# Sparse attention in a tuned model kernel: probabilities scaled before they are turned, values stationary, three branches in one bank

## The reference

```python
for each block of 128 queries, for each of 8 heads (2 groups G of 4):
    p_cmp = masked_softmax(q @ k_cmp * scale)        # 31 compressed keys
    o_cmp = p_cmp @ v_cmp
    p_sel = masked_softmax(q @ k_selected * scale)   # 16 blocks of 64 keys
    o_sel = p_sel @ v_selected
    p_win = masked_softmax(q @ k_window * scale)     # the last 512 keys
    o_win = p_win @ v_window
    o = gate_0 * o_cmp + gate_1 * o_sel + gate_2 * o_win
    o = rms_norm(o, out_norm_g)                      # over 64 elements of a head
y = concat(y_gdn, o) @ w_out
# masked_softmax: exp(s - max) / max(sum, 1e-30)
```

## Time and profile before

| what | value |
|---|---|
| median of the runs | 3776.38 us |
| profiled execution, span | 3785.0 us |
| PE busy | 3658.1 us, 97% |
| PE weight loads | 3036.7 us, 80% |
| DVE busy | 1812.2 us, 48% |
| ACT busy | 1407.3 us, 37% |
| POOL busy | 1403.1 us, 37% |

### The profile page before, as it was taken

How to read it: one execution, slowest core, us unless ns; L and a number is a source line. 1 busy time by engine, 2 the same in 40 slices (tenths; PEclk the granted TensorE clock), 3 DMA queues, 4 the chain that set the end, 5 groups by cost and what they waited for, 6 DMA issues and landing times.

```text
span 3785.0 us, 48784 instructions
## 1 busy us (share of the span) xinstructions
PE 3658.1 (97%) x18948; PEld 3036.7 (80%) x18948; DVE 1812.2 (48%) x3285; ACT 1407.3 (37%) x2037; POOL 1403.1 (37%) x1092
## 2 busy tenths in 40 slices
PE   6999999999999999999899999999999989899998
PEld 5887878777788888888777988888888778898887
DVE  5887416655788664455375441123112457443111
ACT  5665424444322232223255442223222335533222
POOL 2333443233444444444211044454445311114444
PEclk9999999999999999999899999999999989899999
DMA  3211222111355655564300022223222400012222
GB/s 118 78 67 67 92 89 79 56 65 59 131 194 188 215 196 184 182 211 153 84 34 34 12 101 100 85 94 117 95 91 99 134 34 25 33 35 100 98 85 106
DMA packets 67647, 380.25 MB, mean 100 GB/s; under 512 B 7920, under 2 KB 8432, under 8 KB 39408
## 3 DMA queue, kind: packets, MB, share of 16 engines
q1 hardware_dynamic: 44192, 286.14, 21.6%
q10 hardware_dynamic: 23248, 91.19, 7.4%
HBM read 375.20 MB, written 2.10 MB: 100 GB/s over the span
## 4 chain that ended last, share of the span: by engine, by line
PE 46%; issue 30%; POOL 16%; DVE 4%; ACT 2%; DMA 2%; POOLq 0%; ACTq 0%; DVEq 0%
POOL w_lo L350 16%; PE g L385 9%; PE g L379 9%; PE g L380 9%; PE g L364 3%; PE g L365 2%; PE g L366 2%; DMA n_w<-in_w 2%; PE p L1897 1%; PE p L2073 1%; PE p L1863 1%; PE g L1876 1%; PE p L1887 1%; PE p L2079 1%; PE p L1909 0%
## 5 line engine op out<-in xcount | busy, mean ns | idle before, releaser
L350 POOL TENSOR_TENSOR w_lo<-w_raw,w_hi 128x512 fp32r<-128x512 f32 (+1 forms) x1088 | 1402.9, 1321 | 2374.8 <-ACT w_hi L358 2374.8
L379 PE MATMUL g<-h_lo,w_hi 128*128 128x512 f32 x2400 | 949.4, 396 | 3.7 <-ACT w_hi L358 1.6
L380 PE MATMUL g<-h_hi,w_hi 128*128 128x512 f32 x2400 | 935.5, 390 | 0.0
L358 ACT ACTIVATE w_hi<-w_raw 128x2048 fp32r<-128x2048 f32 (+1 forms) x292 | 515.7, 1766 | 948.0 <-PE g L385 859.2
L385 PE MATMUL g<-h_hi,w_lo 128*128 128x512 f32 x2400 | 592.9, 389 | 1.2 <-POOL w_lo L350 1.2
L379 PEld LDWEIGHTS g<-h_lo,w_hi 128*128 128x128 f32 x2400 | 450.8, 188 | 106.3 <-issue 8.6
L380 PEld LDWEIGHTS g<-h_hi,w_hi 128*128 128x128 f32 x2400 | 450.8, 188 | 95.2 <-issue 3.1
L385 PEld LDWEIGHTS g<-h_hi,w_lo 128*128 128x128 f32 x2400 | 450.4, 188 | 95.0 <-POOL w_lo L350 1.6
L379 PE MATMUL g<-act_lo,w_hi 128*128 128x512 f32 x880 | 346.1, 393 | 0.0
L380 PE MATMUL g<-act_hi,w_hi 128*128 128x512 f32 x880 | 343.0, 390 | 0.0
L1650 DVE TENSOR_TENSOR p<-f_acc,g 128x512 f32<-128x512 f32 x84 | 58.4, 696 | 563.7 <-PE g L385 562.5
(11 more groups left out here) (482 smaller groups left out, 5239.4 us busy)
## 6 DMA issues: line engine op xcount, KB each, us to landing
w_raw<-in_stream SPq DMA_DIRECT2D x212, 1024.0 KB, 4.8
ada_w<-in_ada ACTq DMA_DIRECT2D x144, 512.0 KB, 4.0
w_raw<-in_stream SPq DMA_DIRECT2D x80, 704.0 KB, 4.1
n_w<-in_w ACTq DMA_DIRECT2D x8, 1024.0 KB, 18.4
ada_w<-in_stream ACTq DMA_DIRECT2D x8, 512.0 KB, 4.7
x<-in_x SPq DMA_DIRECT2D x4, 512.0 KB, 9.5
b_w<-in_stream ACTq DMA_DIRECT2D x2, 1024.0 KB, 4.8
out_x<-x SPq DMA_DIRECT2D x4, 512.0 KB, 2.6
```

The lines of the kernel that those rows point to most:

```text
L350: last = K.nc.gpsimd.tensor_tensor(K.w_lo[:, s, c], K.w_raw[:, s, c], K.w_hi[:, s, c].bitcast(F32), ALU.subtract)
L358: act.activation(K.w_hi[:, s, 0:width], K.w_raw[:, s, 0:width], ACT.Copy).then_inc(K.sem("w_hi"), 1)
L379: t.matmul(K.g[b][:], K.w_hi[:, s, w], lo[:, k, :], start=starts and i == 0, stop=False)
L380: t.matmul(K.g[b][:], K.w_hi[:, s, w], hi[:, k, :], start=False, stop=False)
```

## The change

The probabilities of the two long branches are scaled before they are turned: row sum and gate are put together into one factor per query (`n_ig` holds the inverse gates, made once per layer), DVE scales group 1 and ACT group 0. The values become the stationary operand and the turned probabilities move, so the result comes out already in rows of channels: 64 for group 0 and 64 for group 1, side by side in one bank of a query block. The compressed branch is two matmuls ahead of each item with i = 0, into the same place, so that nothing has to be added afterwards; the product block before the loop is gone, and so are `added` and the old `squares`. Within a step PE feeds before it turns. `n_p` has three buffers instead of two. After a query block ACT copies the bank to `n_y` (`row_done`). The norm's sums are made after the loop: DVE squares `n_y`, PE adds up over the channels (`squares`), ACT takes the root and DVE the reciprocal on 128 x 512, PE spreads the rows, and DVE multiplies and makes the low part. The rows of `mix_w_out` are put into the new order of channels on the host.

```diff
     def turned(v):
         n = work[v][0] + 1
         for G in range(2):
-            pe.wait_ge(K.sem("n_pe"), pos.next("n_pe"))
+            pe.wait_ge(K.sem(f"n_sc{G}"), pos.next(f"n_sc{G}"))
...
     def weighted(v):
         qb, j, i = work[v]
-        if v >= 2:
-            pe.wait_ge(K.sem("n_acc"), pos.next("n_acc"))
+        q = slice(j * P, j * P + P)
+        if i == 0:
+            if j == 0 and qb >= 2:
+                pe.wait_ge(K.sem("n_yin"), pos.next("n_yin"))
+            for G in range(2):
+                t.matmul(K.p[2 + qb % 2][64 * G:64 * G + 64, q], K.n_bd[:, G, j], K.n_pct[:, 2 * qb + G],
+                         start=True, stop=False)
         for G in range(2):
             pe.wait_ge(K.sem(f"n_tr{G}"), pos.value(f"n_tr{G}") + (1 if v == len(work) - 1 else 0))
-            for k in range(qb + 1):
-                last = t.matmul(K.p[2 + v % 2][:, 64 * G:64 * G + 64], K.n_pt[:, v % 2, 4 * G + k],
-                                K.m_v[:, k, P * i + 64 * G:P * i + 64 * G + 64], start=k == 0, stop=k == qb)
+        for k in range(qb + 1):
+            for G in range(2):
+                last = t.matmul(K.p[2 + qb % 2][64 * G:64 * G + 64, q],
+                                K.m_v[:, k, P * i + 64 * G:P * i + 64 * G + 64], K.n_pt[:, v % 2, 4 * G + k],
+                                start=False, stop=i == 1 and k == qb)
         last.then_inc(K.sem("n_o"), 1)
+
+    def squares():
+        pe.wait_ge(K.sem("n_ysq"), pos.next("n_ysq"))
+        for qb in range(NB):
+            last = t.matmul(K.p[0][32 * qb:32 * qb + 32, :], K.mask("bd64")[:, 48:80], K.n_y2[:, qb],
+                            start=True, stop=True)
+        last.then_inc(K.sem("n_ss"), 1)
...
     for step in range(len(work) + 2):
         if 1 <= step < len(work):
             scores(step)
+        feed(("core", step))
         if 1 <= step <= len(work):
             turned(step - 1)
-        feed(("core", step))
         if step >= 2:
             weighted(step - 2)
...
+    def scaled(v):
+        w = (work[v][0] + 1) * P
+        x = K.n_p[:, v % 3, 0:w]
+        act.wait_ge(K.sem("n_r"), pos.next("n_r"))
+        act.activation(x, x, ACT.Copy, scale=K.n_stat[:, v % 4, 4:5]).then_inc(K.sem("n_sc0"), 1)
...
     for step in range(len(work) + 2):
         if 1 <= step <= len(work):
+            scaled(step - 1)
+        taps(("core", step))
+        if 1 <= step <= len(work):
             turned(step - 1)
         if 1 <= step < len(work):
             probs(step)
-        taps(("core", step))
+        if step in (11, 19, 27):
+            row_done(step // 8 - 1)
...
+    def scaled(u):
+        qb, j, i = work[u]
+        w, r = (qb + 1) * P, s[:, u % 4, 4:6]
+        dve.wait_ge(K.sem("n_pe"), pos.next("n_pe", 2))
+        v.scalar_tensor_tensor(r, s[:, u % 4, 2:4], 1e-30, K.n_ig[:, qb, 1 + 3 * j + i:14 + 3 * j + i:12], ALU.max, ALU.mult
+                               ).then_inc(pos.own, pos.tick())
+        dve.wait_ge(pos.own, pos.ticks())
+        v.reciprocal(r, r).then_inc(K.sem("n_r"), 1)
+        dve.wait_ge(K.sem("n_r"), pos.next("n_r"))
+        x = K.n_p[:, u % 3, w:2 * w]
+        v.tensor_scalar(x, x, s[:, u % 4, 5:6], None, ALU.mult).then_inc(K.sem("n_sc1"), 1)
...
-    for qb in range(NB):
+
+    def y_low(qb):
         q = slice(qb * P, qb * P + P)
         dve.wait_ge(K.sem("yt_hi"), pos.next("yt_hi"))
-        v.scalar_tensor_tensor(K.h_lo[:, 4:8, q], blocks(K.g[qb][:]), K.col2("nsa_g"), K.h_hi[:, 4:8, q].bitcast(F32),
-                               ALU.mult, ALU.subtract).then_inc(K.sem("y2_lo"), 1)
-        dve.wait_ge(K.sem("y2_lo"), pos.next("y2_lo"))
+        v.tensor_tensor(K.h_lo[:, 4:8, q], blocks(K.n_y[:, qb]), K.h_hi[:, 4:8, q].bitcast(F32), ALU.subtract
+                        ).then_inc(K.sem("y2_lo"), 1)
+
+    for qb in range(NB):
+        dve.wait_ge(K.sem("yt"), pos.next("yt"))
+        v.scalar_tensor_tensor(K.n_y[:, qb], K.n_y[:, qb], K.col2("nsa_g"), K.g[qb][:], ALU.mult, ALU.mult
+                               ).then_inc(K.sem("n_yn"), 1)
+        dve.wait_ge(K.sem("n_yn"), pos.next("n_yn"))
         dve.sem_inc(K.sem(f"g_free{qb}"), 1)
+        if qb:
+            y_low(qb - 1)
+    y_low(3)
```

More of the change, by code:

```diff
@@ L2015, in pe_mix @@
     feed("prob")
+    feed("turn")
     pe.wait_ge(K.sem("n_bd"), pos.next("n_bd"))
     pe.wait_ge(K.sem("turned_out"), pos.next("turned_out", 2))
-    for qb in range(NB):
[L2019 to L2026, removed]
     for step in range(len(work) + 2):
@@ L2040, in pe_mix @@
     feed(("z", 0))
+    squares()
     feed(("z", 1))
-    pe.wait_ge(K.sem("n_acc"), pos.next("n_acc", 2))
     for m in range(8):
@@ L2052, in pe_mix @@
         pe.wait_ge(K.sem(f"g_free{qb}"), pos.next(f"g_free{qb}"))
-        pe.wait_ge(K.sem("n_yn"), pos.next("n_yn"))
-        for f in range(4):
-            last = t.transpose(K.g[qb][:, f * P:f * P + P], K.n_y[:, qb, f * P:f * P + P], ident)
+        if qb == 0:
+            pe.wait_ge(K.sem("n_rinv"), pos.next("n_rinv"))
+        for G in range(2):
+            at = 32 * qb + 16 * G
+            last = t.matmul(K.g[qb][64 * G:64 * G + 64, :], ident[:, at:at + 1].broadcast_to([P, 64]), K.n_rr[:],
+                            start=True, stop=True)
         last.then_inc(K.sem("yt"), 1)
@@ L2597, in turned @@
         dve.wait_ge(K.sem("n_pt1"), pos.next("n_pt1"))
+        if u >= 2:
+            dve.wait_ge(K.sem("n_o"), pos.next("n_o"))
         v.tensor_copy(K.n_pt[:, u % 2, 4:4 + n].rearrange("p a b -> p (a b)"), K.p[1][:, 0:n * P]
                       ).then_inc(K.sem("n_tr1"), 1)
[L2601 to L2612, removed]
-        for G in range(2):
-            y = K.n_y[:, qb, (4 * G + j) * 64:(4 * G + j) * 64 + 64]
-            step = v.scalar_tensor_tensor(y, K.p[2 + u % 2][:, 64 * G:64 * G + 64], s[:, u % 4, 4 + G:5 + G], y,
-                                          ALU.mult, ALU.add)
-        step.then_inc(K.sem("n_acc"), 1)
@@ L2619, in squares @@
-    def squares(qb):
-        dve.wait_ge(K.sem("n_acc"), pos.value("n_acc") + 8 * qb + 8)
-        v.tensor_tensor(K.n_ysq[:], K.n_y[:, qb], K.n_y[:, qb], ALU.mult).then_inc(pos.own, pos.tick())
-        dve.wait_ge(pos.own, pos.ticks())
-        v.reduce_sum(K.n_rs[:, 8 * qb:8 * qb + 8], K.n_ysq[:].rearrange("p (h d) -> p h d", h=8), AX
-                     ).then_inc(K.sem("n_ss"), 1)
     for step in range(len(work) + 2):
+        if 1 <= step <= len(work):
+            scaled(step - 1)
         if 1 <= step < len(work):
@@ L2628, in dve_mix @@
             maxima(step)
+        for d in (3, 2):
+            for h in completed(points, ("core", step - d + 1)):
+                tap_of(h, d)
         if 1 <= step <= len(work):
             turned(step - 1)
-        for d in (3, 2, 1):
-            for h in completed(points, ("core", step - d + 1)):
-                tap_of(h, d)
-        if step >= 2:
-            added(step - 2)
-            if step % 8 == 1:
-                squares((step - 2) // 8)
-    pos.skip("n_acc", 32)
+        for h in completed(points, ("core", step)):
+            tap_of(h, 1)
@@ L2639, in dve_mix @@
+    pos.skip("n_o", 2)
     for b in (2, 3):
         dve.sem_inc(K.sem(f"g_free{b}"), 1)
+    dve.wait_ge(K.sem("n_yin"), pos.next("n_yin", 4))
+    for qb in range(NB):
+        last = v.tensor_tensor(K.n_y2[:, qb], K.n_y[:, qb], K.n_y[:, qb], ALU.mult)
+    last.then_inc(K.sem("n_ysq"), 1)
     for n in range(4):
```

52 lines of the change are left out of this document (26 added, 26 removed).

## The result

The changed kernel takes 3798.79 us as the median of nine runs (3786.07 to 3803.83); the kernel before, run beside it, 3780.12 (nine runs, 3771.9 to 3790.7). The ratio is 1.0048, interval 1.0032 to 1.0064: slower by half a per cent, or about 18 us. Run again with twelve runs on another chip it was 1.0030 (1.0013 to 1.0048). The forecast had the sign and under a third of the size: +5.4 for 18.7. The time lies at the very edge of the range that the forecast gave for 8 in 10 (3766 to 3799), and outside the 3776 to 3787 of its own account. The 3776.38 that it stood on was the median of three runs; the nine beside the change gave 3780.12. One execution of the kernel before in experiment 1 took 13543.59 us at a full clock, for a reason that no run shows, and means and ratios leave it out.

A forecast was written before the change was run, and what follows sets the result against it. PE, busy 97% of the span, bounds the kernel. Per layer core −2.0, squares +1.2, DVE after the loop +3.5 make +2.7, +5.4 for two, on 3776.38: 3781.8; own range 3776 to 3787, 8 in 10 3766 to 3799.

The forecast's parts named there:

- rival E: Hand-overs between three engines cost .3 more in fifteen chain-bound steps: +4.5 per layer, 3791; chance .15.
- second .23: Another tiling-switch cost in every PE-bound step, left out of the sum; if due, some 3.7 per layer worse.
- The removed block is thus wholly eaten by its follower: Loop start: product block's 3.65 us goes, yet turned(0) again falls near 1896.05, behind convolution and POOL burst.
- The dip at the start: turned(0) to turned(7): lowered clock in the sparser start, +1.5, instead of the old dip at 1920 to 1925.
- The splits: Weight splits on ACT in steps 15, 23, 31, now between scaling and copying: +1.9, +2.05 with tap, +1.7.
- item 4: turned(23) to turned(31): weighted-sum gains −4.4, POOL +1.1, split of step 31 +1.7; together −1.6.
- Item 5: turned(31) to the loop's end: two last weighted sums −1.2, wait for the copy +.1; together −1.1.
- items 1, 2 and 4: Stretches per layer: turned(0) to turned(7) +2.7; turned(7) to turned(15) −2.1; turned(23) to turned(31) −1.6.
- After the loop: DVE, as bound until the state products, does eight operations instead of four: +3.5 per layer, ends 0 and 5.5.
- Rival C: Column tiles into one bank do not overlap; third and fourth blocks' gains lost, 9.7 per layer: 3801; chance .07.
- Rival B: Chain not caught by POOL, no dip, subtractions half hidden: −3.7 per layer, 3769; chance .21.
- Rival D: Clock falls repeatedly in sixteen chain-bound steps; six more dips +9.4 per layer, 3800 to 3806; chance .15.

The follow-up runs named there:

- experiment 1: Changed kernel again, no edit, on another chip; its profile is the changed kernel's second: 3797.14 to 3783.45 for the kernel before, 1.0030.
- experiment 7: Changed kernel plus 44 dummy products per layer on PE ahead of five turnings where PE waits: 3787.28, 1.0014 of the kernel before.
- experiment 2: Changed kernel with the four low-part subtractions made after the delta rule's products: 3785.12, 1.0003 of the kernel before.
- experiment 3: Changed kernel with item 0's scaling ahead of the last convolution and its split, taps spread over steps 1 to 3: 3791.43, 1.0022.

## Why the prediction was right or wrong

- Bounds, right: PE-bound steps in the third and fourth block, chain-bound ones before. The chain is .11 longer per step than the sum of its rows (2.29 and 2.83 for 2.18 and 2.72), which makes 1.3 us per layer; rival E had .3 a step. The 4.31 of the fourth block is .35 short. It was taken from 4.92, a mean that holds the short step to turned(31), 4.05; steady steps took 5.20. Their gain was .54 and not .61: the weighted sum gained .80 where .72 was forecast, and the turning ahead of the column tiles took back .13. So of the second .23 that the prediction left out about half came.
- "The removed block is thus wholly eaten by its follower", right: turned(0) comes 8.4 us after the compressed branch, 8.5 before, with PE standing for 2.67.
- The dip at the start, right in place and size: +1.5 forecast, 3.85 − 2.29 = 1.56 by experiment 7; the old dip at 1920 went, as said.
- The splits, nearly right: 5.02 against 4.6 (2.72 + 1.9), 6.30 against 6.2 (4.53 before − .38 + 2.05). In item 4 the step behind the split of step 23 and the one with the split of step 31 take 4.65 and 6.37, 11.0 together, against 10.4 (4.53 − .38, 4.05 − .61 + 1.7, and 1.1 for POOL).
- Item 5, "31 to the end", is the step that failed: −1.1 forecast, +.48 measured. With the wait filled the same stretch took 3.25 (experiment 7), the 3.3 of the forecast; a dip of 1.6 comes on it, since PE stands 4.31 ahead of it. The split's wait was in the sum, in item 4; the clock behind it was not.
- The rest of the shortfall: items 1, 2 and 4 were short by .85, 1.2 and 1.0. In items 1 and 2 that is 1.3 for the chain's .11 a step, .4 for the split of step 15 and .3 at the start; in item 4 it is .6 in the two steps at splits and .4 in the steady ones. With item 5's 1.6 that is 4.65, less .45 gained after the loop and .1 ahead of it: the 4.1 between 2.7 and 6.8 in layer 0. So the clock is the largest single miss, and still less than half of it.
- Squares, right: +1.24 for 1.2. After the loop, right: +3.0 for 3.5, and DVE is the bound, since experiment 2 gives all of it back.
- Rival C, wrong: 1.09 for 16 instructions. Rival B, wrong: POOL did catch the chain. The rule of the Trainium skill's "GPSIMD Engine Reference", section 1 (Specifications), that an SBUF interface is shared for vector instructions with two SBUF inputs, held: DVE's subtractions after the loop took 1.36 and .87 under POOL's burst instead of .684.
- Rival D came near the time (3800 to 3806), by luck: it put six more dips per layer into the sixteen chain-bound steps, and the clock is 1.00 from 1910 to 2005 (in layer 0 of the second profile two dips of 1.7 lie there, behind the splits of steps 15 and 23). One more dip than in the forecast lay on the path, worth 1.6 us. Stops as the .28 before 1917.34 don't lower the clock here. The three stops of 2.67, 4.31 and 3.34 us are each followed by a dip. The forecast put a wait in each of the three places, but a dip only behind the first. That dips come again and again stood already in the kernel before: its clock is .80 in the 75 us ahead of the compressed branch.

## What to carry to other kernels

Price a long new wait of the matrix engine twice: once for the wait, and once for the work behind it at the lowered clock. Here the two dips in the loop take 3.2 us of layer 0, where the one that they replace took 1.6, in a loss of 6.8. Compare stages by marks, and clocks over many runs, before believing two spans. An operation that a chain now waits for takes its whole queue along: here a 1.9 us split and a burst on another engine, harmless before, became the stops.

## What the runs showed of the hardware that was not expected

- Executions of one program differ by some 35 us (3765.05 to 3799.58 for the kernel before), and the longer ones have the lower clock (3765.05 at .983, 3799.58 at .973). In the profiles the clock differs most in a stretch with the same work each time.
- A stop of PE doesn't always lower the clock: behind the split of step 23, the same 6.30 step was followed by one of 4.65 in the first profile of the changed kernel and of 5.97 in layer 0 of its second. Nor does it take a stop of 2.67: in experiment 3 a dip of 3.4 came behind stops of 1.15 and .32.
- Useless products in a wait paid for themselves: with 10 us of them per layer, the loop of each layer was 3.2 to 3.7 us shorter.
